# The compressors' first product in a hybrid attention trunk: high and low weight columns in one moving operand

## What is computed

```python
def compress_blocks(x_raw, pe, w1, w2):
    ...
    blocks = x_raw[:, idx] + pe[:, None, :]
    blocks = jnp.moveaxis(blocks, 3, 2).reshape(B, nc, G, CMP_LEN * D)      # (1, 15, 2, 2048)
    return jax.nn.gelu(blocks @ w1, approximate=True) @ w2                  # w1: 2048 x 256, w2: 256 x 64

def even_mixer(h, w_in, w_out, cmp_pe, cmp_w1, cmp_w2):
    ...
    k_cmp = rope(compress_blocks(kv[:, :, 0], cmp_pe[0], cmp_w1[0], cmp_w2[0]), cmp_end)
    v_cmp = compress_blocks(kv[:, :, 1], cmp_pe[1], cmp_w1[1], cmp_w2[1])
```

## Time and profile before

| | |
|---|---|
| median of 3 runs | 656.26 us (656.13 to 656.39) |
| the profiled execution's own time | 656.09 us |
| its span, first to last instruction | 654.3 us |
| TensorE busy | 646.3 us (99%) |
| TensorE weight loads busy | 538.4 us (82%) |
| VectorE busy | 459.5 us (70%) |
| ScalarE busy | 385.5 us (59%) |
| GpSimd busy | 163.7 us (25%) |
| granted TensorE clock | 0.999 of full speed |

### The profile page before, as it was taken

How to read it: one execution, slowest core, us unless ns; L and a number is a source line. 1 busy time by engine, 2 the same in 40 slices (tenths; PEclk the granted TensorE clock), 3 DMA queues, 4 the chain that set the end, 5 groups by cost and what they waited for, 6 DMA issues and landing times.

```text
span 654.3 us, 9977 instructions
## 1 busy us (share of the span) xinstructions
PE 646.3 (99%) x3574; PEld 538.4 (82%) x3574; DVE 459.5 (70%) x627; ACT 385.5 (59%) x561; POOL 163.7 (25%) x123
## 2 busy tenths in 40 slices
PE   9999999999999999999999999999999999999996
PEld 6888887667888888888887888877888888888885
DVE  6498766877697878785457646577688787886532
ACT  7556355865766767666335527565567576767330
POOL 0323300001043443441001001580123434343000
PEclk9999999999999999999999999999999999999999
DMA  8887633005456363637652665104254554545601
GB/s 348 333 304 291 225 129 129 1 6 189 136 191 249 130 245 139 231 154 265 238 196 74 257 223 226 65 2 192 98 195 191 190 194 176 209 154 176 247 1 65
DMA packets 18972, 115.60 MB, mean 177 GB/s; under 512 B 2912, under 2 KB 3454, under 8 KB 6014
## 3 DMA queue, kind: packets, MB, share of 16 engines
q1 hardware_dynamic: 17789, 111.52, 45.6%
q10 hardware_dynamic: 1152, 3.67, 1.6%
HBM read 114.14 MB, written 1.05 MB: 176 GB/s over the span
## 4 chain that ended last, share of the span: by engine, by line
PE 96%; DVE 1%; issue 1%; DMA 1%; ACT 0%; SPq 0%; DVEq 0%; POOLq 0%; POOL 0%
PE ps L1429 27%; PE ps L1436 14%; PE ps L1386 12%; PE ps L1388 12%; PE ps L1387 12%; PE ps L1458 5%; PE ps L1513 2%; PE ps L1757 1%; PE ps L1907 1%; PE ps L1641 1%; PE ps L1891 1%; PE ps L1377 1%; PE ps L1685 1%; DMA raw<-in_weights 1%; PE ps L1920 1%
## 5 line engine op out<-in xcount | busy, mean ns | idle before, releaser
L778 DVE TENSOR_TENSOR wlo<-raw,whi 128x2048 fp32r<-128x2048 f32 x99 | 226.6, 2320 | 71.6 <-ACT whi L413 71.6
L413 ACT CAST whi<-raw 128x2048 fp32r<-128x2048 f32 x99 | 185.9, 1918 | 48.9 <-PE ps L1388 42.0
L1429 PE MATMUL ps<-xpair,whi 128*128 128x512 f32 x768 | 183.4, 391 | 0.0
L1429 PEld LDWEIGHTS ps<-xpair,whi 128*128 128x128 f32 x768 | 141.2, 188 | 27.6
L1436 PEld LDWEIGHTS ps<-xpair,wlo 128*128 128x128 f32 x768 | 98.5, 191 | 3.7
L1436 PE MATMUL ps<-xpair,wlo 128*128 128x256 f32 x768 | 99.6, 283 | 0.0
L1334 POOL TENSOR_TENSOR hidf<-act_g,conv 128x512 f32<-128x512 f32 x22 | 76.0, 3453 | 85.1 <-ACT act_g L671 85.1
L1386 PE MATMUL ps<-whi,hid_hi 128*128 128x512 f32 x176 | 68.5, 389 | 0.0
L1387 PE MATMUL ps<-wlo,hid_hi 128*128 128x512 f32 x176 | 68.5, 389 | 0.0
L1388 PE MATMUL ps<-whi,hid_lo 128*128 128x512 f32 x176 | 68.5, 389 | 0.0
L1386 PE MATMUL ps<-whi,xpair 128*128 128x512 f32 x168 | 67.5, 402 | 0.0
(11 more groups left out here) (197 smaller groups left out, 786.2 us busy)
## 6 DMA issues: line engine op xcount, KB each, us to landing
raw<-in_weights SPq DMA_DIRECT2D x101, 1024.0 KB, 4.9
c_gpost<-in_gpost ACTq DMA_DIRECT2D x4, 512.0 KB, 4.8
raw<-in_weights SPq DMA_DIRECT2D x3, 512.0 KB, 6.7
c_gpre<-in_gpre ACTq DMA_DIRECT2D x3, 512.0 KB, 4.0
h<-in_x SPq DMA_DIRECT2D x2, 512.0 KB, 3.8
out<-h SPq DMA_DIRECT2D x4, 256.0 KB, 2.0
raw<-in_weights SPq DMA_DIRECT2D x2, 256.0 KB, 4.9
t<-in_masks SPq DMA_DIRECT2D x1, 512.0 KB, 12.1
```

What stands on the lines that cost most here:

```text
L413: act.copy(whi[:, slot, :], raw[:, slot, :]).then_inc(hi_done, 1)
L778: dve.tensor_tensor(wlo[:, slot, :], raw[:, slot, :], whi[:, slot, :].bitcast(F32), ALU.subtract).then_inc(lo_done, 1)
L1429: pe.matmul(ps[:, b0 + m, :], whi[:, slot, cols], xpair[:, kt].rearrange("p a c -> p (a c)"), start=kt == 0, stop=kt == KT - 1, skip_group ...
```

## The change

The tiles `whi` and `wlo` become the two halves of one tile `wpair`, at the same place and of the same size. The two products per slice become one, whose moving operand is 2 x 256 columns: the 256 of `whi` and, one tile further (32 KB on in each partition), the 256 of `wlo`. The result takes all 512 columns of the bank: products with the high columns on the left, with the low columns on the right. The halves are added afterwards: ACT copies the right halves of both banks to `hid_lo_half` (in the space of `xbf`, which is no longer needed then) and signals `hid_half`; DVE adds the left halves from PSUM and writes `hid`, and signals `hid_out`. Both stand in the next step, ("unit", 4, 0), behind its split. 64 products of 256 columns become 32 of 512; ACT has as many instructions as before; DVE has one more.

```diff
-        whi = sb("whi", [P, RING, UNIT], F32R)
-        wlo = sb("wlo", [P, RING, UNIT], F32R)
+        wpair = sb("wpair", [P, 2, RING, UNIT], F32R)
+        whi, wlo = wpair[:, 0], wpair[:, 1]
...
+        hid_lo_half = xbf[0:2 * CPAD].rearrange("p a n -> p (a n)")[:, 0:2 * CMP_H].rearrange("p (k c) -> p k c", k=2)
...
-                elif step == ("cmp1", 1, 1):
+                elif step == ("unit", 4, 0):
                     act.wait_ge(unit_used, EVEN_END["cmp1", 1])
-                    act.copy(hid[:], ps[0:2 * CPAD, 6:8, 0:CMP_H]).then_inc(hid_out, 1)
+                    act.copy(hid_lo_half, ps[0:2 * CPAD, 6:8, CMP_H:2 * CMP_H]).then_inc(hid_half, 1)
...
+                elif step == ("unit", 4, 0):
+                    dve.wait_ge(hid_half, 1)
+                    dve.tensor_tensor(hid[:], ps[0:2 * CPAD, 6:8, 0:CMP_H], hid_lo_half, ALU.add).then_inc(hid_out, 1)
...
-                        for part in (whi, wlo):
-                            ins = pe.matmul(ps[0:2 * CPAD, 6 + kind, 0:CMP_H], xb_parts[:, kind, kt, :],
-                                            part[:, u % RING, cols], start=kt == 0 and part is whi,
-                                            stop=kt == CKT - 1 and part is wlo)
+                        ins = pe.matmul(ps[0:2 * CPAD, 6 + kind, :].rearrange("p (a c) -> p a c", a=2),
+                                        xb_parts[:, kind, kt, :], wpair[:, :, u % RING, cols], start=kt == 0,
+                                        stop=kt == CKT - 1)
```

More of the change, by code:

```diff
@@ L235, in build @@
             sem(s) for s in ("x2_turned", "x2_out", "xb_pad", "xb_sum", "xb_hid", "xb_split"))
-        hid_out, hid_turned, hid_gelu, hid_spread = (
-            sem(s) for s in ("hid_out", "hid_turned", "hid_gelu", "hid_spread"))
+        hid_half, hid_out, hid_turned, hid_gelu, hid_spread = (
+            sem(s) for s in ("hid_half", "hid_out", "hid_turned", "hid_gelu", "hid_spread"))
         cmp_ready, kc_prod, kc_rot, vc_out, kc_turned, kc_out = (
```

## The result

| | before | with the change |
|---|---|---|
| median, 14 executions each | 656.22 us | 658.25 us |
| lowest to highest | 656.13 to 657.05 | 656.93 to 659.56 |
| ratio (95% interval) | | 1.0027 (1.0020 to 1.0034) |
| profiled execution, own time | 656.09 us | 658.68 us |
| its span | 654.3 us | 656.9 us |

The change makes the kernel slower by 0.27% (the medians alone differ by 2.03 us, 0.31%). The forecast was 657.1 us with a range up to 657.6, so the result lies above the range. The second line of the table matters as much as the first: the kernel before scatters by 0.9 us with one outlier at 657.05 (the others lie within 0.3), the changed one by 2.6. Its executions form two groups, five from 656.93 to 657.21 and eight from 658.22 to 659.56, with one at 657.79 between them. The profiled execution is from the upper group.

A forecast was written before the change was run, and what follows sets the result against it. PE, busy 646.3 of 654.3 us, was taken to bound the kernel. A 0.15 us saving and 1.01 us from the hidT wait gave +0.86 on 656.09, 656.95, so median 657.1 us; range 656.0 to 657.6.

The forecast's parts named there:

- The products: Compressor steps on PE: 8 products of 512 columns take 1.82 us instead of 1.87, saving 0.19 us in four steps.
- that rival: Compressor products: the moving operand's second run costs time, slower by more than 0.2%, up to 664.3 us; chance 0.06.
- the one of the cheap long product: Compressor products: 512 columns cost less than their columns, a step 0.94 us, total 654.5 us; chance 0.03.
- ScalarE: ACT around the hid copy: the cast fills 2.7 us of idle time, the copy runs at about 64.6; price 0.
- VectorE: DVE behind both splits: the addition runs 71.14 to 71.82, so PE waits about 1.0 us at hidT.
- The no-wait rival: At hidT: the second split ends near 70.1, PE does not wait, only the saving remains, 656.1 us; chance 0.11.
- The delay: Everything behind hidT: -0.15 us saving plus 1.01 us from the wait gives +0.86 us.
- How saving and wait combine: At hidT: PE arrives at 70.67, goes on at 71.72, a 1.05 us gap; everything behind comes 0.86 us later.
- Does something behind take the delay up?: Behind hidT: DVE's idle time clears its backlog, PE's later waits follow PE, so the 0.86 us delay stays.
- another mechanism: Slower by over 0.2%, 0.10: the two-run operand rival, plus 0.04 of the forecast whose hidT wait exceeds 1.5 us.

The follow-up runs named there:

- The three runs with a filled wait: Changed kernel with 1, 2 or 4 products nobody reads queued on PE before the hid_out wait: 657.09, 657.21, 657.30 us.
- the late copy: Kernel before, its 64 products unchanged, but hid copied out of PSUM by VectorE behind both splits: 658.82 us, ratio 1.0035.
- those two kernels: Changed kernel with 1 or 2 products nobody reads added before PE's wait for hid_out: 657.09 and 657.21 us, ratios 1.0012 and 1.0013.

## Why the prediction was wrong

- **The products.** Forecast: 1.82 us per step, 0.19 us in all. Measured: 1.84, 0.12 in all. The fixed part per product is a little smaller than the earlier trace rows suggested, 0.004 us and not 0.006. The estimate by the Trainium skill (TensorE: Matmul & The Clock Gate, Back-to-back issue gap), 0.08 us, came nearer than the rows did. The second run costs about 0.002 us at most: that rival is refuted, and so is the one of the cheap long product.
- **ScalarE.** Right: the cast moved into the idle time (62.73), the copy stayed at 64.53.
- **VectorE.** Right: 71.09 to 71.76 against a forecast of 70.99 to 71.67 (71.14 to 71.82, less the 0.15 by which the chain comes forward), and hidT at 71.82 against 71.72. Most of the 0.1 us is that the chain came forward by 0.06 (first split at 65.59 against 65.65) and not by 0.15. The no-wait rival did not occur.
- **The delay.** Forecast +0.86 us. The three runs with a filled wait give ratios of 1.0012 to 1.0013, 0.8 us (their intervals reach from 0.2 to 1.4 us). The lower group of the changed kernel, 656.93 to 657.26, holds the forecast 657.1. So the sum was right for the executions in which the clock holds.
- **The step that failed** is the pricing of the wait in "How saving and wait combine" and "Does something behind take the delay up?". I set a wait of PE equal to its length, and looked behind it only for idle time that could absorb the delay. I did not ask what PE's idle time does to PE itself. The missing term is the fall of the granted clock to 1.2 GHz for 3.4 us behind the wait, +1.4 to 1.6 us, in most executions (13 of the 22 of the changed kernel lie above 658.2, 12 of them with a mean clock of 0.995 to 0.997). With it the sum is 658.5 to 658.7, and the median of a mixture lies between the groups or in the upper one. The chance of 0.10 for over 0.2% slower was put on another mechanism.
- The evidence that I had was thin but pointed at the right place: PE's waits in the kernel before are at most 0.8 us long, but for the one of 1.3 us at its very start, behind which the clock stays at 1.00. No row showed what a wait of 1 us in the middle costs, so its price needed a bound on both sides, and I gave it none above its length. The Trainium skill (TensorE: Matmul & The Clock Gate, What's actually happening) states the two levels and that inactivity brings the lower one; the trace after agrees with both (1.00 and 0.50, behind 0.99 us without work). That so short a wait can be enough is this measurement's, not the page's. I should have carried it as a rival.

What stays open: why the clock falls in some executions and not in others, with the same wait of about 1 us (the late copy with 0.96 us kept 1.00 in its profile, the changed kernel with 0.99 lost it twice). It is also not shown that the length alone decides: all these waits stand in one place, between 8 transposes and 8 products of 30 columns, and the wait of 1.3 us at the start brings no fall in any profile. One execution of the changed kernel took 658.22 with a mean clock of 1.000 and is not explained by this, and one of the late copy and one of the changed kernel lie between the groups.

## What to carry to other kernels

On a kernel whose TensorE is busy from end to end, price a new wait of TensorE by more than its length: look at the granted clock for some microseconds behind it, and at the scatter of the runs, which splits in two before the median tells anything. When a result moves to another engine, compare its new place in that engine's queue with the moment at which it is needed; here one instruction moved past one split, or six ready products moved ahead of the wait, is worth 2 us. If nothing useful can fill a wait, even one idle product can pay, as it did in this place.

## What the runs showed of the hardware

A single gap of 0.99 us in PE's timeline, in a kernel that is otherwise dense, was followed by 3.4 us at a clock of 0.50. The fall came 1.1 us after the gap in one profile and 2.4 us in the other, while PE was fully busy again. After a gap of 2.32 us the clock was low from about 73.5 us (0.3 us after PE went on) to 80.4. With gaps of 0.75 and 0.53 us it stayed at 1.00, and none of the 22 executions of those two kernels took over 657.7 us. In the 5.6 us without products at the end of the kernel, by contrast, the clock stayed at 1.00 for another 3.0 to 5.4 us before it fell, in all twelve profiles: so the length of a gap does not by itself tell when the clock falls.
